# The last stage of an encoder block rearranged: row loads, row sums, turns and the last down products in another order

## What is computed

```python
r = ALPHA * h + moe(h)                                   # rows gathered from two accumulators
r = r + sigmoid(r @ ple_w_gate) * (p @ ple_w_proj)       # p: 512 x 256, gate: 1024 x 1024
h = layer_norm(r, ln2_g, ln2_b)
```

## Time and profile before

| | us |
|---|---|
| median of 3 runs | 1115.83 (1114.67 to 1116.14) |
| profiled execution, its own time | 1117.09 |
| its span, first to last instruction | 1115.4 |
| TensorE matmul busy | 1072.4 (96%) |
| VectorE busy | 866.0 (78%) |
| ScalarE busy | 709.7 (64%) |
| GpSimd busy | 318.1 (29%) |

### The profile page before, as it was taken

How to read it: one execution, slowest core, us unless ns; L and a number is a source line. 1 busy time by engine, 2 the same in 40 slices (tenths; PEclk the granted TensorE clock), 3 DMA queues, 4 the chain that set the end, 5 groups by cost and what they waited for, 6 DMA issues and landing times.

```text
span 1115.4 us, 15663 instructions
## 1 busy us (share of the span) xinstructions
PE 1072.4 (96%) x5374; PEld 872.4 (78%) x5374; DVE 866.0 (78%) x969; ACT 709.7 (64%) x753; POOL 318.1 (29%) x178
## 2 busy tenths in 40 slices
PE   4999999999999989999999999999999999999896
PEld 3878877778888747888888888888888888887475
DVE  6654346662366687999999999999999999997376
ACT  3431235452143326888888888888888888886253
POOL 1000000000004022444444444444444444442331
PEclk9999999999999999999999999999999999999899
DMA  9432222123366367999999999999999999997811
GB/s 327 150 117 76 76 76 70 45 66 125 113 237 224 116 218 269 368 391 378 385 377 384 386 375 392 383 390 383 381 376 380 384 387 371 390 370 221 297 63 57
DMA packets 72572, 294.82 MB, mean 264 GB/s; under 512 B 15312, under 2 KB 18384, under 8 KB 47696
## 3 DMA queue, kind: packets, MB, share of 16 engines
q1 hardware_dynamic: 52944, 256.43, 59.0%
q0 software_dynamic: 19008, 35.71, 12.5%
q10 hardware_dynamic: 576, 2.10, 0.5%
HBM read 283.67 MB, written 44.04 MB: 294 GB/s over the span
## 4 chain that ended last, share of the span: by engine, by line
PE 89%; DVE 6%; DMA 2%; issue 1%; ACT 1%; SPq 0%; DVEq 0%; POOLq 0%; ACTq 0%
PE ps L414 26%; PE ps L416 25%; PE ps L415 25%; PE ps L1504 5%; DVE w_lo L398 2%; PE ps L1954 1%; PE ps L1528 1%; PE ps L729 1%; PE ps L753 1%; PE ps L740 1%; ACT w_hi L393 1%; DMA xg<-h_rows,get_idx 1%; DMA ln_b<-in_ln_in_b 1%; DMA raw<-in_w_out 1%; DVE x_rows L310 0%
## 5 line engine op out<-in xcount | busy, mean ns | idle before, releaser
L1709 DVE TENSOR_TENSOR w_lo<-gu_raw,w_hi 128x2048 fp32r<-128x2048 f32 x128 | 292.3, 2284 | 5.6 <-ACT w_hi L1594 5.6
L1594 ACT ACTIVATE w_hi<-gu_raw 128x2048 fp32r<-128x2048 f32 x128 | 244.9, 1914 | 3.7 <-DMA gu_raw<-in_moe_w_up 3.5
L414 PE MATMUL ps<-w_hi,xgT_hi 128*128 128x512 f32 x512 | 206.5, 403 | 5.1 <-issue 4.9
L416 PE MATMUL ps<-w_hi,xgT_lo 128*128 128x512 f32 x512 | 201.6, 394 | 0.0
L415 PE MATMUL ps<-w_lo,xgT_hi 128*128 128x512 f32 x512 | 200.9, 392 | 0.0
L1809 POOL DMA_INDIRECT xg<-h_rows,get_idx x64 | 145.7, 2277 | 74.8 <-DVE get_idx L1703 55.1
L414 PE MATMUL ps<-w_hi,act_hi 128*128 128x512 f32 x384 | 154.4, 402 | 2.8 <-DVE act_lo L335 1.4
L1714 DVE TENSOR_TENSOR dn_lo<-dn_raw,dn_hi 128x2048 fp32r<-128x2048 f32 x64 | 146.6, 2291 | 8.2 <-ACT dn_hi L1600 4.7
L416 PE MATMUL ps<-w_hi,act_lo 128*128 128x512 f32 x384 | 150.9, 393 | 0.0
L415 PE MATMUL ps<-w_lo,act_hi 128*128 128x512 f32 x384 | 150.6, 392 | 0.0
L1600 ACT ACTIVATE dn_hi<-dn_raw 128x2048 fp32r<-128x2048 f32 x64 | 122.1, 1908 | 0.0
(11 more groups left out here) (199 smaller groups left out, 1753.8 us busy)
## 6 DMA issues: line engine op xcount, KB each, us to landing
gu_raw<-in_moe_w_gate SPq DMA_DIRECT2D x64, 1024.0 KB
gu_raw<-in_moe_w_up SPq DMA_DIRECT2D x64, 1024.0 KB
dn_raw<-in_moe_w_down SPq DMA_DIRECT2D x64, 1024.0 KB
raw<-in_w_in SPq DMA_DIRECT2D x18, 1024.0 KB, 5.1
h_rows<-x_rows SPq DMA_DIRECT2D x8, 512.0 KB, 5.2
raw<-in_w_out SPq DMA_DIRECT2D x4, 1024.0 KB, 5.6
ple_raw<-in_ple_w_gate SPq DMA_DIRECT2D x4, 1024.0 KB, 10.2
x_rows<-in_x SPq DMA_DIRECT2D x4, 512.0 KB, 10.5
```

Source lines behind the costliest of these rows:

```text
L414: nc.tensor.matmul(out, x_hi, w_hi, start=first, stop=False)
L416: return nc.tensor.matmul(out, x_lo, w_hi, start=False, stop=last)
L1594: nc.scalar.activation(m.w_hi[:, 2 * x.b + half], m.gu_raw[:, 2 * x.b + half], ACT.Copy).then_inc(gu_hi, 1)
L1709: nc.vector.tensor_tensor(m.w_lo[:, 2 * x.b + half], m.gu_raw[:, 2 * x.b + half], m.w_hi[:, 2 * x.b + half].bitcast(F32), ALU.subtract).th ...
```

## The change

In `rounds`, code of the last stage can be given as `finish`; it then follows the first round directly, inside `If(peak <= CAP)`, and a second copy stands behind the later rounds. TensorE passes its whole last stage (`embedding.tensor`), ScalarE and VectorE the first part of theirs (`scalar_weights`, `vector_weights`); the second part (`scalar`, `vector`) comes behind `rounds` as before. SP and GpSimd pass nothing.

For expert 63 the down matrix is split ahead of the silu. TensorE turns h of expert 63 between the two halves of the down product of 62, and down of 63 goes to other PSUM banks (XT), with no wait for `y_ready`. SP loads the first two pieces of the gate matrix right behind p_w, and the other two behind tile 0. The row sums and the low part of piece 0 go from GpSimd to VectorE, the copies of `pp` from VectorE to ScalarE. Tile t + 1 is turned between the two gate units of tile t, and its high and low parts are made there.

```diff
+        if finish is not None:
+            with eng.If(peak[0] <= CAP):
+                finish(eng)
         with eng.If(peak[0] > CAP):
             ...
+            if finish is not None:
+                finish(eng)
...
                 embedding.load_p(sp)
-                sp.wait_ge(y_sum, (r + 1) * NE - 1 + LEAD)
-                embedding.load_weights(sp)
+                embedding.load_weights(sp, 0)
...
-                if at != 0:
+                if at == -1:
+                    down(x.next(-1), halves=(0,))
+                    turn_h(x)
+                    down(x.next(-1), halves=(1,))
+                    down(x, bank=XT)
+                elif at != 0:
                     down(x.next(-1))
             all_experts(pe, r, step)
-            turn_h(Expert(r, QUADS - 1, 3))
-            down(Expert(r, QUADS - 1, 3))
...
-        rounds(pe, body)
-        embedding.tensor(pe)
+        rounds(pe, body, embedding.tensor)
...
-                if at == 0:
+                if at in (0, -1):
                     split_down(x)
                 silu(x)
...
                 if at == -1:
+                    split_hT(x)
                     scale_y(x.next(-1))
             all_experts(act, r, step)
-            split_hT(Expert(r, QUADS - 1, 3))
-            scale_y(Expert(r, QUADS - 1, 3))
+            scale_y(Expert(r, QUADS - 1, 3), bank=XT)
...
-        rounds(act, body)
+        rounds(act, body, embedding.scalar_weights)
         embedding.scalar(act)
...
+                if at == -1:
+                    split_down(x)
                 times_up(x)
...
-        rounds(dve, body)
+        rounds(dve, body, embedding.vector_weights)
         embedding.vector(dve)
...
     def sync(self, sp):
...
-            if t == 1:
-                self.ring.load(sp, 2)
-                self.ring.load(sp, 3)
+            if t == 0:
+                self.load_weights(sp, 1)
...
     def gpsimd(self, pool):
         pool.sem_inc(self.scattered, 1)
-        self.ring.split_lo(pool, 0, nc.gpsimd)
-        for t in range(NT):
-            pool.wait_ge(self.rows_in[t], 32)
-            nc.gpsimd.tensor_tensor(m.x[:, t], m.x[:, t], m.x_odd[t // 2][:, t % 2], ALU.add).then_inc(self.row_sum, 1)
...
-        turn(1)
         for u in range(2 * NT):
...
-            if c == 1 and t + 2 < NT:
-                turn(t + 2)
+            if c == 0 and t + 1 < NT:
+                turn(t + 1)
...
+    def scalar_weights(self, act):
+...
         ring.split_hi(act, 0)
+        copy_pp(0)
         ring.split_hi(act, 1)
-        high_part(0)
-        high_part(1)
+        for u in range(1, 6):
+            copy_pp(u)
+        self.high_part(act, 0)
+        copy_pp(6)
+        copy_pp(7)
         ring.split_hi(act, 2)
         ring.split_hi(act, 3)
...
-            if t + 2 < NT:
-                high_part(t + 2)
+                if u == 2 * t and t + 1 < NT:
+                    self.high_part(act, t + 1)
...
+    def vector_weights(self, dve):
+        ring.split_lo(dve, 0)
+        ring.split_lo(dve, 1)
+        add_rows(0)
+        self.low_part(dve, 0)
+        add_rows(1)
+        ring.split_lo(dve, 2)
+        ring.split_lo(dve, 3)
+        add_rows(2)
+        add_rows(3)
...
     def vector(self, dve):
...
                 self.norm.half_statistics(dve, t, c)
-            if t + 2 < NT:
-                low_part(t + 2)
+                if c == 0 and t + 1 < NT:
+                    self.low_part(dve, t + 1)
```

More of the change, by code:

```diff
@@ L1423, in experts_stage, with rounds @@
     embedding.begin()
-    def rounds(eng, body):
+    def rounds(eng, body, finish=None):
         eng.wait_ge(routing.peak_ready, 1)
@@ L1530, in turn_h, with down @@
             last.then_inc(h_turned, 1)
-        def down(x):
+        def down(x, bank=Y, halves=(0, 1)):
             pe.wait_ge(hT_lo, x.it + 1 + LEAD)
             pe.wait_ge(dn_lo, x.it + 1 + LEAD)
-            pe.wait_ge(y_ready, x.it + LEAD)
-            for c in range(2):
+            if bank == Y:
+                pe.wait_ge(y_ready, x.it + LEAD)
+            for c in halves:
                 for j in range(2):
                     rows, cols = slice(j * CAP, (j + 1) * CAP), slice(j * D + c * 512, j * D + (c + 1) * 512)
-                    last = product3(nc, ps[0:CAP, Y + c], m.hT_hi[:, x.b, rows], m.hT_lo[:, x.b, rows],
+                    last = product3(nc, ps[0:CAP, bank + c], m.hT_hi[:, x.b, rows], m.hT_lo[:, x.b, rows],
                                     m.dn_hi[:, x.b, cols], m.dn_lo[:, x.b, cols], j == 0, j == 1)
-            last.then_inc(y_sum, 1)
+            if halves[-1] == 1:
+                last.then_inc(y_sum, 1)
         def body(r, first):
@@ L1546, in body @@
                     locate(Expert(r, 0, q))
+                pe.wait_ge(y_ready, r * NE + LEAD)
                 turn_x(Expert(r, 0, 0))
@@ L1759, in step @@
                     dve.wait_ge(routing.rows_out, 16 * NT)
-                split_down(x)
+                if at != -1:
+                    split_down(x)
             all_experts(dve, r, step)
@@ L1895, in load_p, with load_weights @@
         sp.dma_start(m.p_w[:], a["ple_w_proj"][0].rearrange("(p j) n -> p (j n)", p=P)).then_inc(self.pw_in, 16)
-    def load_weights(self, sp):
-        self.ring.load(sp, 0)
-        self.ring.load(sp, 1)
+    def load_weights(self, sp, c):
+        self.ring.load(sp, 2 * c)
+        self.ring.load(sp, 2 * c + 1)
     def sync(self, sp):
@@ L2011, in scalar, with low_part, add_rows @@
                 self.norm.centre(act, t)
-    def vector(self, dve):
-        nc, m, ps, ring = self.nc, self.m, self.ps, self.ring
-        def low_part(t):
-            dve.wait_ge(self.hi_done, t + 1)
-            nc.vector.tensor_tensor(m.act_lo[:, :, t * P:(t + 1) * P], self.turned_view(t),
-                                    m.act_hi[:, :, t * P:(t + 1) * P].bitcast(F32),
-                                    ALU.subtract).then_inc(self.lo_done, 1)
-        for t in range(NT):
-            for c in range(2):
-                dve.wait_ge(self.p_sum, 2 * t + c + 1)
-                nc.vector.tensor_copy(m.pp[:, t, c * 512:(c + 1) * 512], ps[:, self.MAIN[c]]).then_inc(self.p_out, 1)
-            if t == 2:
-                dve.wait_ge(ring.lo_split, 1)
-                ring.split_lo(dve, 1)
-                low_part(0)
-        ring.split_lo(dve, 2)
-        low_part(1)
-        ring.split_lo(dve, 3)
+    def low_part(self, dve, t):
+        m = self.m
+        dve.wait_ge(self.hi_done, t + 1)
+        self.nc.vector.tensor_tensor(m.act_lo[:, :, t * P:(t + 1) * P], self.turned_view(t),
+                                     m.act_hi[:, :, t * P:(t + 1) * P].bitcast(F32),
+                                     ALU.subtract).then_inc(self.lo_done, 1)
+    def vector_weights(self, dve):
+        nc, m, ring = self.nc, self.m, self.ring
+        def add_rows(t):
+            dve.wait_ge(self.rows_in[t], 32)
+            nc.vector.tensor_tensor(m.x[:, t], m.x[:, t], m.x_odd[t // 2][:, t % 2], ALU.add).then_inc(self.row_sum, 1)
+        ring.split_lo(dve, 0)
[7 more added lines that the diff above has]
+        add_rows(3)
+    def vector(self, dve):
+        nc, m = self.nc, self.m
         for t in range(NT):
@@ L2036, in vector @@
                 cols = slice(c * 512, (c + 1) * 512)
+                if c == 0:
+                    dve.wait_ge(self.row_sum, t + 1)
+                dve.wait_ge(self.p_out, u + 1)
                 dve.wait_ge(self.gate_ready, u + 1)
```

23 lines of the change are left out of this document (14 added, 9 removed).

## The result

The changed kernel takes 1108.34 us in the median of its runs (1104.75 to 1109.13); the kernel before, run beside it, takes 1114.67 (1112.41 to 1118.6). The ratio is 0.9942, interval 0.9926 to 0.9958: by the ratio 6.5 us less, with bounds of 4.7 and 8.2 (the two medians differ by 6.3). The profiled execution of the changed kernel took 1109.13 us, its span is 1107.4 us against 1115.4 before.

The account below looks back on a forecast made before the run. TensorE, 89% of the chain of waits, was taken as the bound. Act_lo of tile 1 at 1066.1, plus 36.5 and a tail of 8.96, gave span 1111.6, 3.8 us less; applied to the median, 1112.0 us, range 1109.0 to 1115.2.

Parts of the forecast that it names:

- S: Start of SP's first row load behind the last expert's scatter; predicted at 1038.8, bounds 1038.0 to 1040.3.
- L: Time when act_lo of tile 1 is ready, which TensorE awaits ahead of gate unit 2; predicted 1066.1.
- Part 1: Last two experts: down products of 63 follow without idle at full clock and end at 1031.25, 3.45 us earlier.
- Part 2: Products of p: no jump, about 1 us wait for pT, eight units of 1.71 us, ending near 1049.3.
- Part 3: What is late next: VectorE's queue delays act_lo of tile 1, so TensorE idles about 4.5 us at gate unit 2.
- J: VectorE's jump over the later rounds, between its last row add and gate unit 0; 1.7 us, bounds 0.3 to 3.1.
- The clock: TensorE falls to half speed after idling ahead of gate unit 2; charged 1.7 us, bounds 0 and 3.0.
- Part 4: From act_lo of tile 1 ready to the last gate matmul 36.5 us, then an unchanged tail of 8.96.
- B: Rival: short vector chain, with a jump of about 0.3, earlier tile 1 rows or clock kept; 1108.3 us, chance 0.12.
- C: Rival: long vector chain, with a jump of 3.1 us and later tile 1 rows; 1114.7 us, chance 0.21.
- D: Rival: slower, VectorE's far jump needs two fetches in a row, 6.2 us; 1116.5 us, chance 0.07.
- E: Rival: early gate loads starve the scatters, losing the 3.45 us gained at the last experts; 1115.3 us, chance 0.07.

Follow-up runs that it names:

- first half late: Changed kernel with gate-matrix pieces 0 and 1 loaded only after the down product of expert 62; 1107.2 us in one execution.
- row sums where VectorE waits: Changed kernel without VectorE's jump, row sum of tile 2 ahead of tile 0's norm, of tile 3 behind its gain; 1106.18 us, ratio 0.9932 to before.
- the last stage reached by the old jump: Changed kernel without the last-stage copy behind the first round, so TensorE, ScalarE and VectorE jump to it; 1111.27 us, ratio 0.9965 to before.
- second half behind tile 1: Changed kernel with gate-matrix pieces 2 and 3 loaded behind tile 1 instead of tile 0; 1107.44 us in one execution.

## Why the prediction came out as it did

The mechanism was right: faster, by a shorter end of the experts and no jump on TensorE, with a new wait ahead of gate unit 2 whose end is the chain S, rows of tile 1, VectorE, jump, act_lo. The size was too small: 1112.0 us against 1108.34, below the low end of 1109.0. The step that failed is the sum for L, the time at which act_lo of tile 1 is ready: it was 1.85 us too late in the first trace of the changed kernel and 2.98 in the second. Of the 3.7 us by which the time was missed, 1.2 lie in the base, 1115.83 in the first three runs and 1114.67 in all seven; from that base the same forecast is 1110.9 and its low end 1107.8, and the result lies inside the range. The other 2.5 are terms of the sum.

**Part 1** was right for the changed kernel. y of 63 started 5.73 behind the silu (1031.3 in before's time, that is with before's silu at 1025.56; predicted 1031.3), the last down products had no wait, and the scatter came at 1033.2 as predicted. The late scatter of 61 that the bounds allowed for did not come in its two traces; it came in two traces of its variants, for 1.0 and 1.1 us. **S itself was mis-sized**: 1038.05 and 1038.27 in before's time, predicted 1038.8, bounds 1038.0 to 1040.3. I had added 0.2 for a late scatter of 61 and taken 5.36 us from scatter to load, from one trace. The second trace of the kernel before has 4.87, and the eleven with early loads have 4.84 to 5.28, so 5.36 was a high draw.

**Part 2** was right: one wait of 1.01 us for pT, the products at full clock throughout, tile 0 turned at +18.7.

**Part 3.** The wait is where it was predicted and 3.24 and 2.32 us long instead of 4.5. The terms of L:

| term, us | predicted | first trace | second trace |
|---|---|---|---|
| S, in before's time | 1038.8 | 1038.05 | 1038.27 |
| from S to the add of tile 1 | 14.0 | 13.84 | 13.16 |
| J | 1.7 | 1.19 | 0.51 |
| VectorE's work in between and behind | 11.61 | 11.17 | 11.18 |
| L, in before's time | 1066.1 | 1064.25 | 1063.12 |

VectorE's pieces I had summed though they overlap a little. S, landing and J lie within their bounds, S just so, and all four err to one side. J is no fixed number: in the seven traces with a jump at that place the hole was 0.22, 0.39, 0.51, 1.00, 1.19, 1.75 and 1.95 us, two of these (0.51 and 1.19) in the same kernel, and without the jump there was none. The lowest lies below the bounds of 0.3 to 3.1. The Trainium skill, "Advanced Engine Details and Errata", section Control Flow Timing, gives 108 ns for a compare-and-branch; the measured holes are two to eighteen times that. That such a jump waits for a fetch (the Trainium skill, "Runtime: NRT & Kernel Launch", section Instruction fetch mechanics) fits them, but no run here shows the fetch itself.

**The clock.** I charged 1.7 us as if certain. In the two traces of the changed kernel it did fall, and it costs 1.6 (37.0 us against 35.4 from unit 2 to the last sigmoid), so this term is not what was missed there. But a fall is not certain:

| idle of TensorE, us | clock behind it |
|---|---|
| ahead of unit 2: 0.74, 0.99, 1.57 | kept |
| ahead of unit 4: 1.40, 1.50; in the products of p (first half late): 1.65 | kept |
| ahead of unit 4 (row sums where VectorE waits): 1.93 | fell |
| for the jump on TensorE: 2.45 and 2.66 (the kernel before), 3.06 (the last stage reached by the old jump) | fell |
| ahead of the last down products (the kernel before, twice, and last down products as before): 1.98 | fell |
| for pT (VectorE's whole last stage behind the first round): 2.02 | fell |
| ahead of unit 2: 2.32 (the changed kernel, second trace), 2.44 (last down products as before) | fell |
| ahead of unit 2: 2.68 (second half behind tile 1), 2.73 (first half late) | kept |
| ahead of unit 2: 3.24 (the changed kernel, first trace) | fell |

In this stage it was kept behind every idle of up to 1.65 us and fell behind every one of 1.93 us and more, but for the two of 2.68 and 2.73, one execution each. So the wait's length alone does not decide it. The stage of the changed kernel is 5.0 and 6.1 us shorter than before; the timed ratio gives 6.5, with 4.7 in its interval. That a share of its timed executions keeps the clock would fit, but it was not shown, as only profiled ones have a trace.

**Part 4** was 0.6 to 0.7 us short: from L to the last sigmoid 37.2 and 37.1 us against 36.5, although the clock cost 1.6 of them and not 1.7. 0.1 of it is the stall at tile 3 (0.34 instead of 0.25), the rest is not resolved. The tail was right, 8.97 against 8.96. So the stage came out 1.2 us (first trace) and 2.3 (second) shorter than predicted: L too late, less what Part 4 lacked.

**The rivals.** B, 1108.3 us with a chance of 0.12, came closest: a short vector chain. It took J = 0.3, an earlier landing and a clock that is kept. The first two came in part; the clock was not kept in either trace of the changed kernel, so that its number was met is in part luck: S, VectorE's pieces and the base, which it did not name, made up the rest. C and D did not come: no jump on VectorE cost 2 us. E came in small and now and then, and the early loads helped on the whole, as far as one execution without them shows.

What stays open: what makes the lead differ by up to 6 us, what besides the wait decides on the clock, what makes the scatter of 61 land 7.9 to 10.0 us behind its issue, and what sets the hole of the jump between 0.22 and 1.95 us.

## What to carry to other kernels

The first operation behind a far jump starts later by that jump. So follow the program order of each engine across the branch, and either put all of the stage on one side or let the jump fall where the engine waits anyway. Before an engine's order is settled, ask of each instruction who waits for it and what it needs itself: here act_lo stood behind three vector operations that it needs nothing of, and moving it, with the sums and the jump out of the chain, gave nearly as much again as the whole change. When terms of a sum are each taken from one row of one trace, look at how much such a row differs in a second trace of the same kernel: scatter to load was 5.36 and 4.87 us, and the base 1115.83 from three runs and 1114.67 from seven. Together they are 1.7 of the 3.7 us that this forecast missed.

## What the runs showed of the hardware

- The same instructions ahead of the changed stage took 1019.6 to 1025.6 us in 14 traces, while an unchanged stage came again within 0.04 us (89.84 and 89.80). One span beside another says little about 5 us; two stretches cut at the same instruction do.
- TensorE's granted clock fell to half (1.2 GHz) behind idles of 1.93, 1.98 (three times), 2.02, 2.32, 2.44, 2.45, 2.66, 3.06 and 3.24 us. It stayed at full speed behind idles of up to 1.65 us, and behind 2.68 and 2.73.
- The jump over the later rounds left holes of 0.22 to 1.95 us on VectorE in seven traces of nearly the same code, and of 3.06 and 2.32 us on TensorE in the one that jumped there.
- A float32 multiply of 128x512 on VectorE took 0.69 us alone and up to 2.88 us beside GpSimd's shift of 128x1024. The shift took 2.39 us, and 3.23 where it started 0.24 us behind a sum of 128x1024 on VectorE.
- The accumulating scatter of expert 61 landed 6.3 us after its issue in the kernel before (second trace) and 7.9 to 10.0 us with two loads of 1 MB issued ahead of it.
